# Two attention layers on one core: the instructions of all four engines laid in another order

## The reference, cut to what matters

```
for l in range(DEPTH):
    h = rms_norm(x, g_mix[l])
    qa, ka, va, qb, kb, vb, qc, kc, vc, qd, kd, vd, fd = _split_cols(h @ w_in[l])
    oa = stick_breaking_attention(_heads(qa, H), _heads(ka, H), _heads(va, H))
    ob = sliding_window_sink_attention(rms_norm(_heads(qb, H), g_q[l, 0]), rms_norm(_heads(kb, 2), g_k[l, 0]), ...)
    oc = chunked_relpos_attention(rms_norm(_heads(qc, H), g_q[l, 1]), rms_norm(_heads(kc, H), g_k[l, 1]), ...)
    log_f = jax.nn.log_sigmoid(fd + b_f[l])
    od = forgetting_attention(rms_norm(_heads(qd, H), g_q[l, 2]), rms_norm(_heads(kd, H), g_k[l, 2]), ..., log_f)
    groups = [rms_norm(o, g_out[l, i]) for i, o in enumerate((oa, ob, oc, od))]
    x = x + jnp.concatenate(groups, axis=-1) @ w_out[l]
    h2 = rms_norm(x, g_ffn[l])
    x = x + (swiglu(h2, ...) if l == 0 else moe_swiglu(h2, ...))
```

## Time and profile before

| | |
|---|---|
| median of 3 runs | 1521.68 us (1520.24 to 1525.4) |
| profiled execution | 1521.11 us, of which the span is 1519.3 us |
| PE busy | 1470.0 us, 97% of the span |
| DVE busy, ACT busy | 1091.1 us (72%), 907.8 us (60%) |
| POOL busy | 68.9 us |
| attention of layer 0 | about 10 to 170 us of the span |
| attention of layer 1 | about 364 to 520 us |
| experts of layer 1 | about 542 us to the end |

### The profile page before, as it was taken

One profiled execution on the slowest core, in us unless ns is written; L12 is line 12 of the kernel. 1 busy time (PEld: TensorE's weight loads), 2 busy tenths in 40 slices (PEclk: granted clock), 3 DMA queues, 4 the chain that ended last, 5 costly groups with the idle time before them and its releaser, 6 DMA issues.

```text
span 1519.3 us, 16561 instructions
## 1 busy us (share of the span) xinstructions
PE 1470.0 (97%) x6509; PEld 1138.7 (75%) x6509; DVE 1091.1 (72%) x1248; ACT 907.8 (60%) x1206; POOL 68.9 (5%) x102
## 2 busy tenths in 40 slices
PE   7999999999999799999999999999999999999998
PEld 4665688886665577888888888888888888888886
DVE  1344544452234379988998889898899899898896
ACT  2144443341233267777777777787777777777773
POOL 1021000000021101000000000000000000000000
PEclk9999999999999889999999999999999999999999
DMA  8620274429040269999999999999999999999992
GB/s 321 246 111 0 91 265 170 167 85 398 1 154 14 100 247 394 374 365 394 368 372 379 370 362 381 388 364 373 379 357 375 391 366 368 384 360 367 390 384 85
DMA packets 180691, 435.24 MB, mean 286 GB/s; under 512 B 5568, under 2 KB 10368, under 8 KB 180480
## 3 DMA queue, kind: packets, MB, share of 16 engines
q1 hardware_dynamic: 177552, 423.11, 75.3%
q0 software_dynamic: 3056, 11.02, 1.9%
HBM read 428.33 MB, written 5.78 MB: 286 GB/s over the span
## 4 chain that ended last, share of the span: by engine, by line
PE 90%; DVE 6%; ACT 2%; issue 1%; POOL 0%; SPq 0%; DMA 0%; DVEq 0%; ACTq 0%
PE ps L975 13%; PE ps L977 13%; PE ps L976 13%; PE ps L640 8%; PE ps L867 8%; PE ps L869 8%; PE ps L868 8%; PE ps L844 3%; PE ps L845 3%; PE ps L843 3%; DVE unit_rounded L1652 3%; PE ps L763 2%; PE ps L852 2%; PE ps L620 1%; PE ps L734 1%
## 5 line engine op out<-in xcount | busy, mean ns | idle before, releaser
L1652 DVE TENSOR_TENSOR unit_rounded<-wmem,unit_rounded 128x1024 fp32r<-128x1024 f32 (+1 forms) x744 | 854.8, 1213 | 83.2 <-ACT unit_rounded L1207 82.7
L1207 ACT ACTIVATE unit_rounded<-wmem 128x1024 fp32r<-128x1024 f32 (+1 forms) x744 | 719.5, 1042 | 122.9 <-PE ps L977 62.8
L867 PE MATMUL ps<-unit_rounded,vbuf_rounded 128*128 128x512 f32 x528 | 208.8, 396 | 1.4 <-DVE stage_rounded L1663 1.4
L869 PE MATMUL ps<-unit_rounded,stage_rounded 128*128 128x512 f32 x528 | 208.7, 395 | 0.0
L868 PE MATMUL ps<-unit_rounded,vbuf_rounded 128*128 128x512 f32 x528 | 208.7, 395 | 0.0
L975 PE MATMUL ps<-unit_rounded,qkT_rounded 128*128 128x512 f32 x448 | 179.7, 401 | 0.0
L975 PE MATMUL ps<-unit_rounded,hT_rounded 128*128 128x512 f32 x448 | 177.2, 395 | 0.0
L977 PE MATMUL ps<-unit_rounded,qkT_rounded 128*128 128x512 f32 x448 | 177.0, 395 | 0.0
L976 PE MATMUL ps<-unit_rounded,qkT_rounded 128*128 128x512 f32 x448 | 176.9, 395 | 0.0
L977 PE MATMUL ps<-unit_rounded,hT_rounded 128*128 128x512 f32 x448 | 174.6, 390 | 0.0
L976 PE MATMUL ps<-unit_rounded,hT_rounded 128*128 128x512 f32 x448 | 174.5, 390 | 0.0
(11 more groups left out here) (212 smaller groups left out, 1328.1 us busy)
## 6 DMA issues: line engine op xcount, KB each, us to landing
wmem<-in_w_exp_gate_dram SPq DMA_DIRECT2D x56, 2048.0 KB, 8.8
wmem<-in_w_exp_up_dram SPq DMA_DIRECT2D x56, 2048.0 KB, 9.1
wmem<-in_w_exp_down_dram SPq DMA_DIRECT2D x56, 2048.0 KB, 9.3
wmem<-in_w_in_dram SPq DMA_DIRECT2D x4, 3072.0 KB, 17.6
wmem<-in_w_ff_gate_dram SPq DMA_DIRECT2D x5, 2048.0 KB, 9.1
wmem<-in_w_ff_up_dram SPq DMA_DIRECT2D x5, 2048.0 KB, 7.9
wmem<-in_w_ff_down_dram SPq DMA_DIRECT2D x5, 2048.0 KB, 8.8
wmem<-in_w_out_dram SPq DMA_DIRECT2D x4, 2048.0 KB, 19.2
```

Of the source, the lines that this page charges most:

```text
L867: pe.matmul(o, hhb, hi[:, b, c], start=(first and b == 0), stop=False, skip_group_check=True)
L869: mm = pe.matmul(o, hlb, hi[:, b, c], start=False, stop=(b == blocks - 1), skip_group_check=True)
L1207: act.activation(quarter_r(HIGH[l][0 if last else kind], q, cols), quarter(SETS[l][i][kind], q, cols), ACT.Copy).then_inc(hi_ready[kind], 1)
L1652: dve.tensor_tensor(quarter_r(u, q, cols), quarter(u, q, cols), quarter_r(HIGH[l][0 if last else kind], q, cols), ALU.subtract).then_inc(l ...
```

## The change

No operation is added and none is taken away; the same products, transposes and reads stand in another order. `FILLS` and the new list `PROJECTIONS` are written out by hand, a projection can be issued in halves of four products, transposes of the weights come by single heads, the output projection comes by single steps, and DVE's, ACT's and POOL's lists are rewritten to match. Some helpers are split so that their parts can stand apart. `p_ready` counts one for A instead of four, with the waits changed to match. Of the three `attention` functions in the diff the first is PE's (from its middle on), the second ACT's (its end), the third DVE's (from C's keys on).

```diff
-FILLS = [("x", i) for i in range(4)]
-for _i, _g in enumerate(ORDER):
-    FILLS += [(_g, "qk", 0), (_g, "qk", 1)]
...
+FILLS = [
+    ("x", 0), ("x", 1), ("x", 2), ("x", 3), ("D", "qk", 0), ("D", "qk", 1), ("A", "qk", 0), ("A", "qk", 1),
...
+PROJECTIONS = [
+    ("D", 0), ("D", 1), ("A", 0), ("D", 2), ("D", 3), ("A", 1), ("A", 2), ("A", 3), ("C", 0), ("C", 1), ("C", 2),
+    ("B", 0), ("B", 1), ("C", 3)]
...
             def attention(l):
...
+                project(l, "C", 2, (0,))
+                values(l, "D")
+                qk_transposes(l, "C", 0)
                 stick_sums(l)
-                project(l, "C", 3)
-                values(l, 1, "A")
...
+                qk_transposes(l, "C", 1)
+                project(l, "B", 0, (0,))
+                project(l, "C", 2, (1,))
+                scores(l, "C")
+                values(l, "A")
...
+                p_transposes(l, "C", 2)
+                qk_transposes(l, "B", 0)
+                project(l, "C", 3, (0,))
+                p_transposes(l, "C", 3)
+                project(l, "C", 3, (1,))
+                qk_transposes(l, "B", 1)
+                o_transposes(l, "A")
+                out_project(l, 0, "D", 0)
...
+                o_transposes(l, "B")
+                out_project(l, 0, "D", 1)
+                out_project(l, 0, "B", 0)
+                out_project(l, 0, "B", 1)
+                out_project(l, 1, "A", 1)
+                out_project(l, 1, "B", 0)
+                out_project(l, 1, "B", 1)
                 norm(l, "y", (0, 1))
-                out_project(l, 1, ["B"])
                 emptied(pe, l, ("y", 0))
                 emptied(pe, l, ("y", 1))
...
             def attention(l):
...
+                if l == 0:
+                    norm_square(l, "y", 0)
+                    norm_read(l, "y", 0)
+                    norm_read(l, "y", 1)
+                    norm_square(l, "y", 1)
...
+                else:
+                    norm_square(l, "y", 0)
+                    norm_square(l, "y", 1)
+                    norm_read(l, "y", 1)
+                    norm_read(l, "y", 3)
...
             def attention(l):
...
+                group_read(l, "D")
+                group_squares(l, "D")
+                scale_qk(dve, l, 2, "C", 0)
+                group_scale(l, "D")
+                stick_logits(l)
+                softmax_logits(l, "C")
+                softmax_max(l, "C")
```

More of the change, by code:

```diff
@@ L644, in qk_transposes @@
-            def qk_transposes(l, gi, g):
-                nb = 3 if g == "B" else 4
[L646 to L652, removed]
+                if 0 in halves:
+                    if m < NT:
+                        emptied(pe, l, ("x", 2 * m))
+                        emptied(pe, l, ("x", 2 * m + 1))
+                    if m >= 2:
+                        pe.wait_ge(pr_free[m % 2], l * (NPF // 2) + m // 2)
+                    if u == 0:
+                        pe.wait_ge(s_win[g], 16 * (l + 1))
+                    if u == 2 and g == "D":
+                        pe.wait_ge(s_wd[1], 16 * (l + 1))
@@ L746, in o_transposes, with out_project @@
                 mm.then_inc(tr_full, 1)
-            def out_project(l, t, groups):
-                if groups[0] == ORDER[0]:
+            def out_project(l, t, g, kk):
+                first, last = (g, kk) == FIRST_OUT[t], (g, kk) == LAST_OUT[t]
+                if first:
+                    for i in range(2):
+                        pe.wait_ge(s_wo[i], 16 * (l + 1))
                     if t == 0:
@@ L753, in out_project @@
                             pe.wait_ge(pr_free[(NPU + b) % 2], l * (NPF // 2) + (NPU + b) // 2)
-                        for i in range(2):
-                            pe.wait_ge(s_wo[i], 16 * (l + 1))
                     else:
                         wait_scores_free(l, "out")
[L758 to L768, removed]
+                emptied(pe, l, (g, "oT"))
+                k = 2 * CAT[g] + kk
+                for half in range(2):
+                    mm = pe.matmul(ps[:, 2 * t + half, :], oT[:, t, k * P:(k + 1) * P], wo[:, k, half * 512:(half + 1) * 512],
+                                   start=first, stop=last)
+                    if last and t == 0:
+                        mm.then_inc(pr_full, 1)
+                if last and t == 1:
                     mm.then_inc(sc_full, 1)
@@ L1055, in _, with norm_read @@
         def _(act):
-            def norm(l, name):
+            def norm_read(l, name, i):
                 y = name == "y"
                 parts = y and l == 0
[L1060 to L1085, removed]
-                    act.wait_ge(gains, 1)
-                    for t in range(NT):
-                        read(2 * t + 1)
@@ new lines, in norm_square @@
+            def norm_square(l, name, t):
+                y = name == "y"
+                if y and t == 0:
+                    act.wait_ge(pr_free[0], (l + 1) * (NPF // 2))
+                    act.wait_ge(pr_free[1], (l + 1) * (NPF // 2))
+                elif y:
+                    act.wait_ge(sc_free, (l + 1) * NSU)
+                elif l:
+                    act.wait_ge(x_added, 2 * (t + 1))
+                else:
+                    act.wait_ge(s_x[t], 16)
+                act.activation(squares[y][t], x[:, t, :], ACT.Square, accum_out=ssx[:, t:t + 1]).then_inc(ssx_ready, 1)
@@ L1429, in norm_read @@
                     return
-                for i in [2 * t for t in ts]:
+                for i in parts:
                     t = i // 2
```

539 lines of the change are left out of this document (312 added, 227 removed), and 4 rows, old and new, of the table FILLS.

## The result

| | before | changed |
|---|---|---|
| median | 1520.96 us (1520.04 to 1525.4, 4 runs) | 1493.24 us (1492.94 to 1493.56, 4 runs) |
| profiled execution, span | 1521.11, 1519.3 us | 1493.56, 1491.8 us |

The ratio is 0.9824, 95% interval 0.9807 to 0.9841: 27.5 us less between the two profiled executions, where 27.5 were forecast, though not quite by the same sum.

What follows compares the result with a forecast made beforehand. PE, busy 97% of the span, was the bound, so only its idle time and slow clock could be won. Gains of 14.5 (layer 0) and 15.0 (layer 1) less 2 for margins made 27.5 us: 1494 us, range 1485 to 1506.

Steps and rivals of the forecast that it cites:

- The windows without waits: Both attentions, from second half of D's first projection to the output projection's end: 134.4 us in each layer without waits.
- restarts and clock: Layer 1's attention window: sixteen waits cost 4.3 us beyond idle, at 0.27 each; half clock lost 0.9 us.
- Thin margins: Both layers' attention: 1 us charged in each layer for thin margins that don't hold.
- the stage of B: B's norm, squares to last read of a B unit: 3.81 us under 4.45 of PE work, margin 0.6.
- A's scaling: On DVE behind B's norm, 0.62 us; transposes of A's output need it 0.3 us later, margin 0.3.
- The stick chain: A's chain over DVE, ACT and PE, sums to A's values: needs 6.3 us under 7.4, margin 1.1.
- The new wait at the feed-forward part: Layer 0's end: reads take 4.0 us from the first transpose; PE waits about 3.2, plus 0.9 for the clock.
- The router: Layer 1's end: about 14.0 us from last product to router's end at half clock, before 11.15; loss 2.85.
- Late readers: Attention: three chains each late by about 1.7 us, 5 us a layer in place of 1: 1501.6 us; chance 0.20.
- A clock that stays full: Both layers' ends: no half clock, 0.9 and 4.4 us come back: 1488.3 us; chance 0.11.
- Idle time that only moves: PE's in-order waits reappear elsewhere, 12 us a layer on top of the main case: 1518 us; chance 0.04.
- slower: A's chain over DVE, ACT and PE becomes the bound; 18 us late in each layer gives 1527 us; chance 0.03.

Runs made afterwards that it cites:

- eighth run: Changed kernel with four DVE sums that nobody reads (about 2.45 us) ahead of DVE's scaling of B's second tile, both layers: 1498.02 us.
- seventh: Changed kernel with one DVE sum that nobody reads (about 0.6 us) ahead of DVE's scaling of B's second tile, both layers: 1493.78 us.
- fifth experiment: Changed kernel with A's values ahead of B's half unit and C's scores, close behind the sums: 1503.72 us.
- sixth run: Changed kernel with all six halved projections joined to whole units, all else in its order: 1494.64 us.
- fourth: Changed kernel with D's start in the old order, D's values ahead of A's first unit, sums directly ahead of D's transposes and scores: 1498.99 us.

## Why the prediction came right, term by term

**The windows without waits.** Forecast 134.4 us of work in each layer with the transposes of the new x (0.87), so 133.53 without: measured 133.53 and 133.54. (I had named 134 to 138 as the sign to look for; the transposes of the new x have left the window, and it is 0.5 us under that.) The idle time, 11.8, was read from the profile and is right. That the rest closed to 0.01 us is luck: two of its terms were off and cancel. I had read the earlier trace rows, 0.57 of full clock over 4 us, as 1.7 us at half clock and 0.9 lost. A mean of 0.57 means 3.4 us at half and 1.7 lost, as shorter windows show; the second is a stretch of layer 0 that explains its 1.6 us more:

```profile
400.10:403.40 3.30, 3.30 (x12) 1.76 (x10) 1.62 (x1) 0.00 (x0) 0.00 (x0) 0.50 0.00 0
150.90:154.30 3.40, 3.40 (x7) 1.62 (x7) 1.81 (x7) 0.00 (x0) 0.89 (x2) 0.50 0.00 0
```

And layer 1's window of the earlier trace rows ends with the tail of the last product (519.90), 0.15 us behind the start of the router (519.75). Of the 5.2 us that I took off for restarts and clock, 1.7 are the clock and 0.15 this tail; 3.4 are left for sixteen restarts, 0.21 each and not 0.27. Measured singly, a restart is 0.24 us (eighth run).

**Thin margins, 2 us in all.** Not needed: the windows have no wait at all. Of the three margins two were as worked out: the stage of B is done at 450.14 and asked for at 450.61 (0.5 for 0.6), A's scaling at 450.65 and 450.94 (0.3 for 0.3). Here are DVE and then PE at this place:

```profile
449.86 0.28 DVE L1543 COPY vbuf<-ps 128x128 f32<-128x128 f32 x1
450.05 0.60 DVE L1659 TENSOR_SCALAR obuf<-obuf,ro 128x256 f32<-128x256 f32 x2
```

```profile
450.61 0.49 PE L653 MATMUL ps<-con,stage 128*128 128x128 f32 x3
450.94 0.60 PE L747 MATMUL ps<-con,obuf 128*128 128x128 f32 x4
```

That 0.5 us is cover is what the eighth run shows: a stage late by 1.58 us costs what the margin leaves over, once. The seventh shows that 0.6 us more work on DVE costs nothing where DVE idled 0.7.

**The stick chain.** Its margin was 2.3 us, not 1.1: the exponential ends at 429.71, the values begin at 431.99. I took 2.85 us from the end of the mask to the end of the exponential from the earlier trace rows; now it is 1.5 (428.20 to 429.71), since ACT loaded the exponential's table ahead of its wait for the mask. On ACT's timeline:

```profile
426.18 1.28 ACT L1174 ACT_TABLE_LOAD   x1
428.23 1.48 ACT L1174 ACTIVATE wmem<-wmem 128x1536 f32<-128x1536 f32 x1 [0.77 <-DVE wmem L1766]
```

The two traces differ in one more thing at this load. In the kernel before, the wait is an instruction of its own (L1143) that ends at 448.4, just ahead of the load; in the changed one no such instruction is recorded, and the wait is the activation's. The view of its line, with its times in the two layers:

```profile
L1143 ACTq EVENT_SEMAPHORE  x2: 17/17/17, 96.6 to 448.4; - x2
```

The fifth experiment prices the cover: without it 2.5 and 2.8 us of waiting, and clock on top.

**The new wait at the feed-forward part.** 4.0 us from the first transpose, measured 4.07 (150.74 to 154.81). The clock behind it cost 1.7 us, not 0.9, by the same misreading of the earlier trace rows: from 155.5 to 158.5 the products came 0.43 us apart in place of 0.23, and from L871 to the second half of D's first projection in layer 1 it took 200.66 us, where the sixth run, which began at full clock, took 198.98.

**The router.** From the last product to its end 13.79 us (489.00 to 502.79), 2.64 more than before, for 2.85. The half clock lasted further into the gather L962 than before, 6.26 us for 5.41: 0.85 that I had not counted.

**Layer 0's start.** The second half of D's first projection began at 17.20 in place of 16.70. Nothing ahead of it was changed in any kernel, and over the ten profiled executions it began between 16.16 and 17.80. The eight products before it took 5.0 to 6.4 us in place of 3.5, at a granted clock of 1.00 and with the transfers at full load; what spreads them is open.

**The sum as measured.** Layer 0: the same place of layer 1 is reached 13.0 us sooner (368.49 and 355.47), for 14.5 less 1 of the margins. Layer 1: 17.9 - 2.64 - 0.85 = 14.4, for 15.0 less 1. Together 27.4, and 27.5 between the spans. The large terms were right, and that the small ones met so closely is luck: 2.0 us of margins not needed and 0.2 at the router on one side; the start, the clock and the gather, 0.5 + 0.8 + 0.85 = 2.2, on the other.

**The rivals.** Late readers (1501.6): out, no late read at all, though DVE's scaling of D did take 1.14 us beside POOL's table:

```profile
425.39 1.14 DVE L1659 TENSOR_SCALAR obuf<-obuf,ro 128x256 f32<-128x256 f32 x2 [0.31 <-POOL ro L1382]
426.45 1.75 DVE L1766 TENSOR_TENSOR wmem<-ps,con 128x1536 f32<-128x1536 f32 x1
```

The mask behind it ran beside the table too and took 1.75 us, as without it (1.76 in the earlier trace rows); it has one input in the result banks. The rule that I had named (the Trainium skill, SBUF — State Buffer, section "SBUF: two separate sides") says that only a VectorE instruction in a two-port mode, or with two inputs in SBUF, competes with GpSimd for the shared ports; that fits both rows, though no row says in which mode the scaling ran, and I had charged the mask as well. A clock that stays full (1488.3): right in neither layer of the profiled execution, though in the fourth and sixth experiments layer 0's feed-forward part did begin at 1.00. Idle time that only moves, and slower: out, as the windows show.

**What the prediction left out.** The best end was not the one of the change. The new end costs 4 to 7 us on the kernel before and, undone well, gives 5 to 7 us on the changed kernel; the sum had both end terms as losses and did not ask what the same order with the old end would give.

## What to carry to other kernels

An in-order matrix engine that is 97% busy still lost 12 of 152 us a layer to waits of 0.3 to 2.0 us, and 5 more to restarts and a half clock behind them: list each wait, and put long blocks that need nothing new between an operation's operands and its use. Walk the new order with durations from the trace; a margin of 0.5 us held, and in the profiled execution a reader that missed it cost its overrun and 0.24 us, once. Three of that kernel's five executions were 3 us slower still, at a lower mean clock. Do the same at the ends: transposes that feed the next stage want two steps behind them to cover their reads (two steps ahead of them still left 0.3 us of wait), and a term of the sum that is a loss is a place to change before the kernel is run.

## What the runs showed of the hardware

A change of half a per cent can hide in the clock. The kernel before took 1517.91 to 1525.8 us in nine runs on one chip, and its mean granted clock went from 0.993 to 0.988 and 0.987 as the time went up. The stretch at half clock behind a wait is not fixed: behind the same 3.04 us wait of the feed-forward part it was there in the changed kernel (0.72 granted over 6 us) and not in the sixth run, and in the fifth experiment it lasted about 7 us in layer 1, behind a wait of 2.8 us, and 3.4 in layer 0, behind one of 2.5. What decides it these runs don't show. A table load on ACT (1.28 us) can stand on either side of the wait of the instruction that needs it: behind it in the kernel before (448.44, after 5.94 us of waiting for the mask), ahead of it in the changed one, for the same operation. Where it came behind, the wait was an instruction of its own; what makes the wait one, these runs don't show. A chain's time should be worked out with the load and without.
